# The multilayer part as seven products of halves for eight

## The reference

```
hn = rmsnorm(x, mlp_norm_g)
hid = jnp.square(jax.nn.relu(jnp.einsum('bsd,df->bsf', hn, w_up)))      # 1024 x 1024 by 1024 x 4096
x = x + jnp.einsum('bsf,fd->bsd', hid, w_down)                          # 1024 x 4096 by 4096 x 1024
```

## Time and profile before

| | us |
|---|---|
| median of 3 runs | 2884.48 (2883.9 to 2888.43) |
| profiled execution | 2882.69 |
| its span | 2880.8 |
| of it from 2178.1, the multilayer part | 702.7 |
| TensorE busy | 2755.9 (96%) |
| VectorE busy | 1505.5 (52%) |
| ScalarE busy | 1202.0 (42%) |
| GpSimd busy | 538.1 (19%) |

### The profile page before, as it was taken

One profiled execution on the slowest core, in us unless ns is written; L12 is line 12 of the kernel. 1 busy time (PEld: TensorE's weight loads), 2 busy tenths in 40 slices (PEclk: granted clock), 3 DMA queues, 4 the chain that ended last, 5 costly groups with the idle time before them and its releaser, 6 DMA issues. The chain is left out here.

```text
span 2880.8 us, 37468 instructions
## 1 busy us (share of the span) xinstructions
PE 2755.9 (96%) x13996; PEld 2299.6 (80%) x13996; DVE 1505.5 (52%) x2332; ACT 1202.0 (42%) x1930; POOL 538.1 (19%) x439
## 2 busy tenths in 40 slices
PE   8999999988999999999999998799999999999999
PEld 7887766777888888888888887788887888888887
DVE  5770375457424888888887687456533112022021
ACT  3111243666422577777775312556432213122130
POOL 0222112100230122222220121000021222222221
PEclk9999999998999999999999999899999999999999
DMA  3123124211452699999995320000211111111112
GB/s 131 44 79 130 44 81 148 85 41 56 148 194 89 230 373 383 389 376 376 365 370 212 126 59 15 1 1 1 75 66 37 57 50 41 55 49 51 48 48 81
DMA packets 134425, 374.94 MB, mean 130 GB/s; under 512 B 24080, under 2 KB 46352, under 8 KB 109712
## 3 DMA queue, kind: packets, MB, share of 16 engines
q1 hardware_dynamic: 117056, 339.48, 33.3%
q0 software_dynamic: 10656, 20.99, 2.1%
q10 hardware_dynamic: 6576, 12.58, 1.2%
HBM read 341.54 MB, written 49.28 MB: 136 GB/s over the span
## 5 line engine op out<-in xcount | busy, mean ns | idle before, releaser
L635 POOL TENSOR_TENSOR w_lo<-w_raw,w_hi 128x512 fp32r<-128x512 f32 (+2 forms) x252 | 315.5, 1257 | 1504.0 <-ACT w_hi L614 1503.1
L614 ACT ACTIVATE w_hi<-w_raw 128x512 fp32r<-128x512 f32 (+2 forms) x252 | 148.4, 599 | 852.0 <-PE banks L687 831.1
L2386 DVE TENSOR_TENSOR w_lo<-w_raw,w_hi 128x2048 fp32r<-128x2048 f32 x192 | 437.1, 2293 | 64.6 <-ACT w_hi L2320 60.3
L2320 ACT ACTIVATE w_hi<-w_raw 128x2048 fp32r<-128x2048 f32 x187 | 355.8, 1925 | 39.4 <-PE banks L2445 39.4
L687 PE MATMUL banks<-act_hi,w_hi 128*128 128x512 f32 x768 | 301.3, 392 | 8.1 <-ACT stage L911 3.7
L687 PE MATMUL banks<-act_lo,w_hi 128*128 128x512 f32 x768 | 300.6, 391 | 0.0
L687 PE MATMUL banks<-act_hi,w_lo 128*128 128x512 f32 x768 | 300.5, 391 | 0.0
L687 PE MATMUL banks<-w_hi,act_hi 128*128 128x512 f32 (+1 forms) x576 | 217.7, 378 | 7.0 <-DVE act_lo L1721 3.2
L687 PE MATMUL banks<-w_lo,act_hi 128*128 128x512 f32 (+1 forms) x576 | 217.3, 377 | 0.0
L687 PE MATMUL banks<-w_hi,act_lo 128*128 128x512 f32 (+1 forms) x576 | 217.3, 377 | 0.0
L2443 PE MATMUL banks<-w_hi,xT 128*128 128x512 f32 x512 | 205.1, 401 | 0.5 <-DVE xT L2391 0.5
(11 more groups left out here) (496 smaller groups left out, 5566.4 us busy)
## 6 DMA issues: line engine op xcount, KB each, us to landing
w_raw<-in_w SPq DMA_DIRECT2D x192, 1024.0 KB, 7.4
w_raw<-in_w_in SPq DMA_DIRECT2D x72, 256.0 KB, 2.7
w_raw<-in_w_up SPq DMA_DIRECT2D x64, 256.0 KB, 2.8
w_raw<-in_w_down SPq DMA_DIRECT2D x64, 256.0 KB, 2.6
scratch_gateT<-gate_staged SPq DMA_DIRECT2D x32, 256.0 KB, 2.1
gate<-scratch_gateT SPq DMA_DIRECT2D x32, 256.0 KB, 3.3
gate_raw<-in_w_in SPq DMA_DIRECT2D x15, 512.0 KB, 4.4
y_rows<-scratch_y SPq DMA_DIRECT2D x7, 1024.0 KB, 5.0
```

The source lines that it names most:

```text
L614: act.activation(v.w_hi[:, i % RING, :cols], v.w_raw[:, i % RING, :cols], ACT.Copy).then_inc(hi_done, 1)
L635: pool.tensor_tensor(v.w_lo[:, i % RING, :cols], v.w_raw[:, i % RING, :cols], v.w_hi[:, i % RING, :cols].bitcast(F32), ALU.subtract).then_ ...
L2320: act.activation(hi[c % SLOTS][:, :], raw[c % TILES][:, :], ACT.Copy).then_inc(hi_done, 1)
L2386: dve.tensor_tensor(lo[c % SLOTS][:, :], raw[c % TILES][:, :], hi[c % SLOTS][:, :].bitcast(F32), ALU.subtract).then_inc(lo_done, 1)
```

## The change

The up and the down product of each part of 1024 hidden columns are each a "round" (8 rounds, up in even r, down in odd r). Every 1024 x 1024 by 1024 x 1024 product is cut into quarters of 512 x 512 and made of seven products of quarters or of sums of quarters (Winograd's form of Strassen's scheme), where before there were eight. Operand a is the activations (x in up rounds, hid in down rounds), b the weights. Products 0 to 6 of a round take a from 11, S1, S2, S4, S3, 12, 22 and b from 11, T1, T2, 22, T3, 21, T4, where S and T are sums and differences of quarters made in place by VectorE.

A product is made in two halves of its inner dimension, each called q in the code (14 a round): high and low parts of a and b of 128 x 1024 elements, each in a ring of three. ScalarE makes the high parts and squares and rectifies; VectorE makes the low parts of a, the S and T, all bank additions, and the low parts of b except those of q = 4, 6, 8, 10, 12 of a round, which GpSimd makes. In round 0 each a part (1 MB) is also stored to DRAM, and rounds 2, 4 and 6, whose a is the same x, load it back and make none. A product uses four banks, and the next but one uses the same. In down rounds the quarters of the residual sum up products; four products are summed apart over the rounds (in round 1 ScalarE copies them), and joined to the residual at the end by 16 additions ahead of the last four bank additions. The weights are loaded in quarters of 1 MB, four slots. The output is stored in 8 stores of 512 KB. In the tail of the stage before, the turned rows are copied once (to `xT`), without a low part, and the first half of product 0 is split there.

```diff
+class Rounds:
+    A, B, C = ("11", "S1", "S2", "S4", "S3", "12", "22"), ("11", "T1", "T2", "22", "T3", "21", "T4"), ("11", "22", "12", "12", "22", "11", "21")
+    SUMMED_APART = (0, 1, 2, 4)
+    PARTS, RING, PRODUCTS = 14, 3, 7
+    POOL_PARTS = (4, 6, 8, 10, 12)
+    COUNT = 2 * DFF // D
+    DONE_ORDER = ("12", "22", "11", "21")
...
+        self.x = at("xT", ACTS, [P, ND, S])
+        self.slot = [at(f"w_quarter{i}", kb, [P, 4, N]) for i, kb in enumerate((RINGS, RINGS + 8, RINGS + 16, FREE + 56))]
+        self.a = [at(f"a_parts{i}", kb, [P, 2, 2, N], F32R) for i, kb in enumerate((FREE, ACTS + 32, ACTS + 40))]
+        self.b = [at(f"b_parts{i}", kb, [P, 2, 2, N], F32R) for i, kb in enumerate((FREE + 8, ACTS + 48, ACTS + 56))]
+        self.totals = at("totals", ACTS, [P, 4, 4, N])
+        self.hid, self.sums = at("hid", FREE + 16, [P, ND, S]), at("sums", FREE + 48, [P, 4, N])
...
+    def of(self, q):
+        return q // self.PARTS, q % self.PARTS // 2, q % 2
+    def up(self, r):
+        return r % 2 == 0
+    def makes_a(self, r):
+        return r == 0 or not self.up(r)
+    def copies(self, g):
+        r, p = divmod(g, self.PRODUCTS)
+        return p in ((0, 1) if self.up(r) else self.SUMMED_APART if r == 1 else ())
+    def spent(self, q):
+        return (self.ready, 4 * (q // 2 + 1)) if q % 2 else (self.used, q // 2 + 1)
+    def read(self, g, h):
+        return (self.copied, self.n_copied[g] + h + 1) if self.copies(g) else (self.summed, self.n_summed[g] + h + 1)
+    def banks(self, g, h):
+        return self.v.pair[2 * (g % 2) + h].rearrange("p (u c) -> p u c", c=N)
...
+    def b_high(self, act, q):
+        r, p, _ = self.of(q)
+        if q >= self.RING:
+            act.wait_ge(*self.spent(q - self.RING))
+        if self.B[p][0] == "T":
+            act.wait_ge(self.b_added, self.n_b_added[q + 1])
+        else:
+            self.wait_weights(act, r, self.B[p])
+        act.activation(self.b[q % self.RING][:, :, 0, :], self.b_source(q), ACT.Copy).then_inc(self.b_hi, 1)
+    def a_high(self, act, q):
+        r, p, h = self.of(q)
+        if not self.makes_a(r):
+            return
+        if q >= self.RING:
+            act.wait_ge(*self.spent(q - self.RING))
+        if self.RING <= q < self.RING + self.PARTS:
+            act.wait_ge(self.stored[q % self.RING], 16 * (q // self.RING))
+        if self.A[p][0] == "S":
+            act.wait_ge(self.a_added, self.n_a_added[q + 1])
+        else:
+            self.wait_squared(act, r, self.A[p], h)
+        act.activation(self.a[q % self.RING][:, :, 0, :], self.a_source(q), ACT.Copy).then_inc(self.a_hi, 1)
+    def of_pool(self, q):
+        return q % self.PARTS in self.POOL_PARTS
...
+    def wait_lows(self, eng, q):
+        for s, n in self.lows(q):
+            if n:
+                eng.wait_ge(s, n)
+    def b_low(self, dve, q):
+        if self.of_pool(q):
+            return
+        x = self.b[q % self.RING]
+        dve.wait_ge(self.b_hi, q + 1)
+        dve.tensor_tensor(x[:, :, 1, :], self.b_source(q), x[:, :, 0, :].bitcast(F32), ALU.subtract).then_inc(self.b_lo, 1)
+    def b_low_pool(self, pool, q):
+        x = self.b[q % self.RING]
+        pool.wait_ge(self.b_hi, q + 1)
+        pool.tensor_tensor(x[:, :, 1, :], self.b_source(q), x[:, :, 0, :].bitcast(F32), ALU.subtract).then_inc(self.b_lo_pool, 1)
+    def a_low(self, dve, q):
+        if self.makes_a(self.of(q)[0]):
+            x = self.a[q % self.RING]
+            dve.wait_ge(self.a_hi, self.n_a_made[q + 1])
+            dve.tensor_tensor(x[:, :, 1, :], self.a_source(q), x[:, :, 0, :].bitcast(F32), ALU.subtract).then_inc(self.a_lo, 1)
+    def b_add(self, dve, q):
+        r, p, h = self.of(q)
+        name = self.B[p]
+        if name[0] != "T":
+            return
+        left, right = {"T1": ("12", "11"), "T2": ("22", "11"), "T3": ("22", "12"), "T4": ("21", "11")}[name]
+        self.wait_weights(dve, r, left)
+        self.wait_weights(dve, r, right)
+        self.wait_lows(dve, q - 2)
+        out = self.b_source(q)
+        dve.tensor_tensor(out, self.weights(r, left, h), out, ALU.subtract).then_inc(self.b_added, 1)
+    def a_add(self, dve, q):
+        r, p, h = self.of(q)
+        name = self.A[p]
+        if name[0] != "S" or not self.makes_a(r):
+            return
+        x = self.x if r == 0 else self.hid
+        out = self.a_source(q)
+        dve.wait_ge(self.a_lo, self.n_a_made[q - 1])
+        if name == "S1":
+            for part in ("21", "22"):
+                self.wait_squared(dve, r, part, h)
+            ins = dve.tensor_tensor(out, self.quarter(x, "21", h), self.quarter(x, "22", h), ALU.add)
+        elif name == "S2":
+            self.wait_squared(dve, r, "11", h)
+            ins = dve.tensor_tensor(out, out, self.quarter(x, "11", h), ALU.subtract)
+        elif name == "S4":
+            self.wait_squared(dve, r, "12", h)
+            ins = dve.tensor_tensor(out, self.quarter(x, "12", h), out, ALU.subtract)
+        else:
+            ins = dve.tensor_tensor(out, self.quarter(x, "11", h), self.quarter(x, "21", h), ALU.subtract)
+        ins.then_inc(self.a_added, 1)
...
     def sync(sp):
         last.load(sp)
         sp.wait_ge(ready, NT)
-        v.mlp_ring.load_first(sp, v.mlp_tiles)
+        for name in ("11", "12", "22"):
+            w.load(sp, 0, name)
     def scalar(act):
-        def high(t):
+        def copy(t):
             for h in range(2):
                 act.wait_ge(last.turned, 2 * t + h + 1)
-                act.activation(part(v.act_hi, t, h), bank(t, h), ACT.Copy).then_inc(hi_done, 1)
+                act.activation(part(w.x, t, h), bank(t, h), ACT.Copy).then_inc(made, 1)
         last.high(act)
         for t in range(NT):
             last.square(act, t)
             if t:
-                high(t - 1)
-            if t == 2:
-                v.mlp_ring.high_first(act)
-        high(NT - 1)
+                copy(t - 1)
+            if t == 4:
+                act.wait_ge(last.lo_done, ND)
+                w.b_high(act, 0)
+                act.wait_ge(made, 2 * 4)
+                w.a_high(act, 0)
+        copy(NT - 1)
     def gpsimd(pool):
         last.low(pool)
-        v.mlp_ring.low_first(pool)
     def vector(dve):
-        _, then = chain(dve, link)
-        def low(t):
-            for h in range(2):
-                dve.wait_ge(hi_done, 2 * t + h + 1)
-                dve.tensor_tensor(part(v.act_lo, t, h), bank(t, h), part(v.act_hi, t, h).bitcast(F32), ALU.subtract).then_inc(lo_done, 1)
+        _, then = chain(dve, sem("dve_link"))
         for t in range(NT):
             last.add(dve, t)
             last.norm(dve, then, t)
-            if t:
-                low(t - 1)
-        low(NT - 1)
+            if t == 5:
+                dve.wait_ge(last.lo_done, ND)
+                w.b_low(dve, 0)
+                w.a_low(dve, 0)
     def tensor(pe):
         for t in range(NT):
             last.multiply(pe, t)
             if t:
-                last.turn(pe, t - 1, lo_done)
-        last.turn(pe, NT - 1, lo_done)
+                last.turn(pe, t - 1, made)
+        last.turn(pe, NT - 1, made)
     return Tail(sync, scalar, gpsimd, vector, tensor)
...
+    copies_at, rectified_at, sums_at = {}, {}, {}
+    for g in range(w.COUNT * PRODUCTS):
+        r, p = divmod(g, PRODUCTS)
+        at = 2 * p + 4 - (w.up(r) and p >= 5)
+        (copies_at if w.copies(g) else sums_at).setdefault(r * PARTS + at, []).append(g)
+        if w.up(r) and p >= 3:
+            rectified_at.setdefault(r * PARTS + (11, 12, 13, 15)[p - 3], []).append(g)
...
+        def _(sp):
+            w.load(sp, 0, "21")
+            for r in range(w.COUNT):
+                for i in range(PARTS):
+                    q = r * PARTS + i
+                    kept = d["x_parts"][i]
+                    if r == 0:
+                        sp.wait_ge(w.a_lo, q + 1)
+                        sp.dma_start(kept, w.a[q % RING_][:, :, :, :].bitcast(F32)).then_inc(w.stored[q % RING_], 16)
+                    elif w.up(r):
+                        if r == 2 and i == 0:
+                            for n in range(RING_):
+                                sp.wait_ge(w.stored[n], 16 * len(range(n, PARTS, RING_)))
+                        sp.wait_ge(*w.spent(q - RING_))
+                        sp.dma_start(w.a[q % RING_][:, :, :, :].bitcast(F32), kept).then_inc(w.a_landed[q % RING_], 16)
+                    if r + 1 < w.COUNT and i in (10, 13):
+                        w.wait_lows(sp, r * PARTS + (9 if i == 10 else 13))
+                        for name in (("11", "12") if i == 10 else ("22", "21")):
+                            w.load(sp, r + 1, name)
+        @block.scalar
+        def _(act):
+            def copy(g):
+                r, p = divmod(g, PRODUCTS)
+                act.wait_ge(w.a_lo, w.n_a_made[r * PARTS])
+                for h in range(2):
+                    act.wait_ge(w.ready, 4 * g + 2 * h + 2)
```

(179 more changed lines are left out.)

137 lines of the change are left out of this document (61 added, 76 removed).

## The result

The changed kernel takes 2813.31 us (median of 4 runs, 2811.93 to 2822.02) against 2884.19 us: a ratio of 0.9763, with a 95% interval of 0.9735 to 0.979. Beside it on other chips the ratio was 0.9739 (0.9708 to 0.9769) and 0.9761 (0.9748 to 0.9775). The forecast was 2832 us, in a range of 2815 to 2862: right in its sign, and some 19 us short of the gain. The profiled execution took 2811.96 us, its span 2810.1.

A forecast was written before the change was run, and what follows sets the result against it. TensorE's matmul count was taken as the bound; -87.0 matmuls, +23 stalls, +11.6 end, +0.5 last stores, -0.7 start gave -52.6 us. From 2882.69 that is 2830.1, plus 1.8 to the median: 2832 us, range 2815 to 2862.

The forecast's parts named there:

- Matmuls, -87.0: Last stage: 2688 matmuls instead of 3072 at 0.2267 us each, 87.0 us less.
- Stalls in all: 23 us: All TensorE waits in the last stage, clock loss included: 23 us, from 8 to 45 or 50.
- Inside rounds 3, 5, 7: GpSimd's low parts hold VectorE's, so TensorE loses 1.5, 0.8 and 0.7 us at parts 3, 5 and 7.
- a dozen handovers 1 us: Even to odd round: part 2's low parts are ready just when due, and handovers between engines lose 1 us.
- Round 0 to 1: Round 0 also makes a, so TensorE waits at its end and into round 1: 11 us with clock and handovers.
- the clock's 2: After the 3.5 us stall at round 1's start, TensorE may run at 1.2 GHz: 2 us added.
- The further 1.7 and 1.5 at parts 2 and 3: Round 1: TensorE loses 1.7 us at part 2 and 1.5 us at part 3.
- The end: +11.6: Kernel end: 16 joins and four bank additions leave VectorE 12.3 us behind TensorE instead of 0.7, +11.6 us.
- DMA at 0: Rounds 2, 4, 6 read a back and round 0 stores it, all in time: cost 0, at most 18 us.
- Rival 2: GpSimd's hold falls on waits VectorE has anyway, or is shared; losses at parts 3, 5, 7 go: 2821 us, chance 0.13.
- Rival 1: VectorE is the bound in rounds that make a, with 45 us of stalls: 2854 us, chance 0.20.
- The 6 us a round: GpSimd's five low parts and VectorE's two-input instructions exclude each other, adding 6 us to VectorE's load each round.

The follow-up runs named there:

- odd-parts kernel: Against the changed kernel, GpSimd makes the low parts of b at q = 3, 5, 7, 9, 11 instead of 4, 6, 8, 10, 12: 2832.98 us, ratio 0.9821.
- the fused one: Against the changed kernel, relu and square of products 5 and 6 in up rounds are one VectorE instruction instead of two on ScalarE: 2814.5 us, ratio 0.9756.
- rounds made anew: Against the changed kernel, rounds 2, 4 and 6 make all their a parts themselves, with nothing stored to DRAM or read back: 2829.26 us, ratio 0.9807.
- kernel with two matmuls of three: Against the changed kernel, TensorE leaves out the high x high product, 32 matmuls for 48 in each product: 2746.08 us.
- 32 cases by themselves: Two standalone runs, 16 cases each, of GpSimd's low part against 12 VectorE instructions: GpSimd took 3.05 to 3.25 us, then 2.35 to 3.38 us.
- joined-twice kernel: Against the changed kernel, totals of rounds 1, 3, 5 are joined in round 6 and five pairs of joins come earlier in round 7: 2804.08 us, ratio 0.9739.

## Why the prediction was right, and where it was off

- Matmuls, -87.0: right, as the spacing (0.2267 us) is the same after the change. Count and spacing came from the trace, and TensorE stayed the bound.
- The step that failed is the size of "Stalls in all: 23 us", measured 4.3. Of it, "Inside rounds 3, 5, 7 [...] GpSimd's part 4 begins at about 13.7, just ahead of VectorE's lows of part 3" gave 1.5, 0.8 and 0.7 a round, 9 us with round 1's fourth part apart; none came. GpSimd did begin there (2427.43) and did conflict, but waited 5.5 us for VectorE; the later holds, 2.1 to 2.2 us each as priced, met VectorE with slack enough, if only just at part 7. The mechanism is real (the odd-parts kernel pays 18 us for it), the order of service was wrong. It is not the whole of the 9 us: VectorE also stood 1.1 us earlier in the round than I had it (lows of part 3 ready 14.9 us into round 3, for 16.0). Had GpSimd been served at the next boundary, 2428.38, these lows would have ended at about 2431.8 for a part due at 2431.0, and with VectorE's row unbroken to part 7, those of part 7 about as late: an estimate from these rows of some 1.5 us a round, half of the 3.0. Nor did "a dozen handovers 1 us" come: the lows of part 2 in round 3 end at 2425.06, 0.5 before they are due.
- Round 0 to 1: 11 us were forecast; the waits at part 13 and at part 0 came, with 0.8 and 2.8 for 1.7 and 3.5, and the clock's 2 as 1.4. The further 1.7 and 1.5 at parts 2 and 3 did not; at part 2 that is luck of a kind, since the spell had made TensorE late, and the kernels that lost the spell waited there (1.24 us without GpSimd's low parts, 2.44 in the fused one). The chain of relu, square, high and low part is borne out by the fused kernel and by the rounds made anew.
- The end: +11.6 against +9.8 measured, shown by the kernel without joins. DMA at 0: right, no wait for a load, with part loads of 4.8 us; they bind only in the kernel with two matmuls of three, behind VectorE's low parts.
- Rival 2 (the hold falls on waits that VectorE has anyway) described what happened best, and its 2821 us was nearer. I gave it 0.13 since the earlier trace rows show a neat hold; they show the price of one, not where the next will fall. Rival 1's load of VectorE was right as a sum (471 us in the stage) and wrong as a bound.
- The Trainium skill's rule ("SBUF — State Buffer", "Who interferes with whom") that the two exclude each other whole agrees with the traces of the changed and the odd-parts kernel: no GpSimd low part ran beside a two-input VectorE instruction. That whichever starts first goes first does not: GpSimd's from 2427.43 stood behind four VectorE instructions issued after it, and the measurement decides. The 6 us a round, 46 in all, that the forecast added to VectorE for this came to some 5 in all (50 to 52 us of holds against 46 saved), since 27 or 28 of the 40 met an instruction and the rest a gap or a bank addition, and they cost TensorE nothing.

Open: why GpSimd is passed over at four or five boundaries at q = 4 of rounds 1, 3, 5 and 7 (7.8 us, the same in every profile of the changed kernel), at q = 4 of round 0 (5.4 to 5.6 us) and at times at q = 8 of round 1, and never in 32 cases by themselves. What its yielding saved in rounds 3, 5 and 7 is read from the order of the rows and estimated; no kernel here forced it to be served there.

## What to carry to other kernels

A conflict priced from one row is a price, not a loss: lay each hold on the timeline and ask whether the held instruction is the one that the bound engine waits for. Moving the same helper work by one part here cost 18 us, and dropping it nothing. Chains that cross a stage boundary (bank addition, relu, square, split) and rows of work left for the end are paid in full; spread the latter into rounds where the engine is light, but not in front of the last operands.

## Not expected of the hardware

A wait's length alone doesn't say whether a spell at 1.2 GHz follows: one came after 2.82 us in the changed kernel and after 2.7 us in the odd-parts kernel, none after 2.75 us in round 7 of the joined-twice kernel, nor after 2.44 us in the fused one. One came even after 1.84 us, in round 1 of the odd-parts kernel, and none after 2.82 us before round 3 of the kernel that makes its a anew. Each spell lasted 3.4 us and cost 1.4 to 1.6, by the starts of its matmuls. And a ScalarE release at eight points of VectorE's pitch gave GpSimd durations that fall from 2.9 to 2.35 us in steps of 0.1 and then jump to 3.38: by itself, it waits out the rest of the running instruction and no more.
